# A streaming encoder on one core: the band's far corner masked by added contraction rows, turns over all 128 rows, and the bias reversed beside the latent heads

## The chip, the core and the metric

The kernel runs on one core of a Trainium2 chip. Its engines work side by side: TensorE (PE, with its weight loads PEld), VectorE (DVE), ScalarE (ACT), GpSimd (POOL) and SyncE (SP, which here issues every DMA). Each has its own instruction stream, and they order each other by semaphores. The metric is the time of one execution in microseconds of device time.

## The reference

One inference step of a two-layer trunk, for 1024 prompt frames and 64 sample frames that share all weights (model width 1024, chunks of 64 frames). The first layer runs two head groups from one projection: an mLSTM matrix memory (4 heads of 128) and a latent attention (8 heads). The second layer runs band attention with 16 heads of 64. Each layer ends in a SwiGLU FFN. What the change touches is in the band attention and, for the reversed bias, beside the latent attention:

```
def band_attend(q, k, v, q_pos, k_pos, rel_bias):
    s = einsum('bqhd,bkhd->bhqk', q, k) * C_SCALE
    idx = clip(q_pos[:, None] - k_pos[None, :], -MAX_REL, MAX_REL) + MAX_REL
    s = s + rel_bias[:, idx]
    qc, kc = (q_pos // CHUNK)[:, None], (k_pos // CHUNK)[None, :]
    valid = (k_pos[None, :] >= 0) & (kc <= qc) & (kc >= qc - LEFT_CHUNKS)
    p = softmax(where(valid, s, -inf))
    return einsum('bhqk,bkhd->bqhd', p, v)
```

With chunks of 64 and 8 chunks to the left, a tile of 128 queries sees five tiles of 128 keys, and in the farthest one the corner of the second 64 queries against the first 64 keys is outside the band: the far corner. It exists for query tiles 4 to 7.

## The kernel before, in words

The program is a row of stages (`load`, `in0`, `gate`, `mlstm`, `latent`, `heads`, `mla`, `out0`, `ffn0`, `in1`, `band`, `out1`, `ffn1`, `final`); a stage ends with its semaphores cleared and a barrier of all engines, and each stage holds one hand-written instruction stream per engine. Order within a stage is the order of these streams, and their waits.

**Latent attention (`mla_stage`).** Eight heads, nine query tiles each (`TILES`), in pairs: pair 0 written out, pairs 1 and 2 in a loop, pair 3 written out. For each tile PE scores, DVE takes the maximum, ACT exponentiates, PE turns the weights, ACT keeps them, PE weighs V. SP's stream loads q and k of the first two heads (`load(0)`, `load(1)`), then per head the V of the next head (`load_v`), and, after ACT, DVE and POOL have split the next head's q and k (`wait_split`), the q and k of the head after that. ACT's `split_q` (L1562) is the first that waits for such a load; it stands in ACT's stream between the exponentials. At the end of SP's stream `turn_bias` (L1365) copies the relative bias reversed into `relT` (L1369, one element at a time in reverse order), waits for it, spreads it into `biasT` (L1372), and waits for that.

**Band attention (`band_stage`).** Sixteen heads; those of a pair share 128 output rows, e = h % 2. A head has 13 pieces (`PIECES`, index i): eight key tiles against the queries that see them, cut at 512 queries, and the sample last. Key-major scores of a piece are two matmuls, `k2` by `q2` over 128 rows and `k3` by `q3` over H + 1 = 65 rows (row 64 carries a one against the negative row maximum), then two matmuls with `biasT`, and, in pieces i = 5, 7, 9 and 11, one matmul over a single row of `halves` that puts the mask on the far corner (L1925). ACT exponentiates a piece (L2022; the sample in two, L2017 and L2019), and PE weighs V with it two pieces later (L1948; the sample L1943, whose last key tile has 64 rows).

The row maxima of the next head are found beside the pieces of this one: at i = 4 to 12 PE computes the scores of query tile t = i - 4 once more, query-major, in `peak` (L1869; for tiles 4 to 7 with a one-row `halves` matmul for the corner), and DVE reduces them (L2099). `peak(h, t)` waits until DVE has reduced tile t - 1. PE then turns the maxima into rows (`rows`, L1888, the sample's over 64 rows) and ACT writes them into row 64 of `q3` (`keep_row`). PE also turns the next head's V (L1822), K (L1832, five turns over 64 rows, and the sample's V, L1833) and cached K (L1838); ACT takes the K (`take_k`) before PE may turn the cache. DVE has, in between, the divisions of the heads of the pair before or of this one (`divide`, L2114 a reciprocal and L2117 a product; `QUOTIENT_AT` places four of them at i = 7 to 10 of odd heads and five at i = 3, 5, 7, 9, 11 of even heads), `split_q`, `take_v` (L2089), `split_c` and `keep_tot`. At the stage's start DVE fills constants (eight instructions, `set_up`), and PE waits for them before the first `peak`.

In fp32 a matmul leaves two weight loads and two matmul records in the trace; a transpose leaves one of each.

## Time and profile before

| what | value |
|---|---|
| median of three runs | 3591.8 us (3588.12 to 3599.15) |
| the profiled execution: its time, its span | 3594.18 us, 3592.4 us |
| PE busy over the span | 3259.7 us (91%) |
| DVE, ACT, POOL busy | 1100.4, 888.6, 918.5 us (31%, 25%, 26%) |
| mean granted TensorE clock | 0.948 of full speed |

The span runs from the first to the last instruction of the profiled execution; its time has 1.8 us more. A PE record starts when the engine takes it up and its end is modelled, so the distance from one start to the next says more than the duration. The number in brackets at the end of a row is idle time of that engine before the instruction, with what ended it; "issue" is idle time in which the engine waited for nothing that the profile shows.

### The profile page before, as it was taken

How to read it: one execution, taken by the hardware profiler on the slowest of the kernel's cores; microseconds unless marked ns; L12 is line 12 of the kernel's file. 1: busy time of each engine (PE TensorE's matmuls, PEld its weight loads, DVE VectorE, ACT ScalarE, POOL GpSimd, SP SyncE). 2: the span in 40 equal slices, each digit the busy share in tenths (PEclk: the TensorE clock that was granted, in tenths of full speed). 3: DMA queues.
4: the chain of work that ended last, by engine and by line, in shares of the span. 5: the costliest groups of instructions: out<-in, count | busy, mean ns of one | idle time of the engine just before them, and what ended most of it. 6: DMA issues, size and time to landing. Idle time of an engine off the chain costs nothing. (4 is left out here: it accounts for less than half of the span.)

```text
span 3592.4 us, 49644 instructions
## 1 busy us (share of the span) xinstructions
PE 3259.7 (91%) x19284; PEld 3070.4 (85%) x19284; DVE 1100.4 (31%) x2155; ACT 888.6 (25%) x1626; POOL 918.5 (26%) x604
## 2 busy tenths in 40 slices
PE   6996558899889999999989997999988999999998
PEld 5996337788879999999979995777777999999998
DVE  3112662454131221222141113555522212211223
ACT  3001422554131221212130002444322212111211
POOL 3211102110142322232232113444313323222320
PEclk8998678899989999999999997999989999999999
DMA  3222414315121111111002215334312111111101
GB/s 105 97 90 101 109 47 163 77 47 52 47 70 36 59 47 35 35 58 47 0 30 95 92 73 137 81 79 85 76 36 70 48 35 37 56 47 35 47 23 56
DMA packets 194784, 229.78 MB, mean 64 GB/s; under 512 B 61631, under 2 KB 167312, under 8 KB 194464
## 3 DMA queue, kind: packets, MB, share of 16 engines
q1 hardware_dynamic: 194688, 228.51, 22.3%
q8 instruction: 60, 0.98, 0.1%
q14 instruction: 36, 0.29, 0.0%
HBM read 181.92 MB, written 54.44 MB: 66 GB/s over the span
## 5 line engine op out<-in xcount | busy, mean ns | idle before, releaser
L237 PE MATMUL ffn_banks<-hhi,ffn_whi 128*128 128x384 f32 (+1 forms) x2112 | 691.6, 327 | 20.2 <-POOL hlo L218 13.2
L239 PE MATMUL ffn_banks<-hhi,ffn_wlo 128*128 128x384 f32 (+1 forms) x2112 | 691.2, 327 | 0.0
L238 PE MATMUL ffn_banks<-hlo,ffn_whi 128*128 128x384 f32 (+1 forms) x2112 | 691.1, 327 | 0.0
L237 PEld LDWEIGHTS ffn_banks<-hhi,ffn_whi 128*128 128x128 f32 x2112 | 399.1, 189 | 21.7 <-issue 21.7
L238 PEld LDWEIGHTS ffn_banks<-hlo,ffn_whi 128*128 128x128 f32 x2112 | 398.9, 189 | 0.0
L239 PEld LDWEIGHTS ffn_banks<-hhi,ffn_wlo 128*128 128x128 f32 x2112 | 398.7, 189 | 0.0
L891 POOL TENSOR_TENSOR ffn_wlo<-ffn_stage,ffn_whi 128x2048 fp32r<-128x2048 f32 x66 | 303.5, 4611 | 357.8 <-ACT ffn_whi L851 357.8
L237 PE MATMUL in_banks<-hhi,in_whi 128*128 128x384 f32 (+1 forms) x1104 | 362.8, 329 | 22.5 <-issue 13.6
L957 DVE TENSOR_TENSOR ffn_act<-ffn_silu,ffn_banks 128x384 f32<-128x384 f32 x132 | 70.1, 532 | 962.7 <-PE ffn_banks L239 946.3
L239 PE MATMUL in_banks<-hhi,in_wlo 128*128 128x384 f32 (+1 forms) x1104 | 362.3, 328 | 0.0
L238 PE MATMUL in_banks<-hlo,in_whi 128*128 128x384 f32 (+1 forms) x1104 | 362.0, 328 | 0.0
L963 DVE TENSOR_TENSOR xT<-xT,ffn_banks 128x384 f32<-128x384 f32 (+1 forms) x528 | 281.0, 532 | 240.4 <-PE ffn_banks L239 240.4
L239 PE MATMUL ffn_banks<-ffn_ahi,ffn_wlo 128*128 128x384 f32 (+1 forms) x1056 | 344.2, 326 | 0.0
L238 PE MATMUL ffn_banks<-ffn_alo,ffn_whi 128*128 128x384 f32 (+1 forms) x1056 | 344.1, 326 | 0.0
L237 PE MATMUL ffn_banks<-ffn_ahi,ffn_whi 128*128 128x384 f32 (+1 forms) x1056 | 344.0, 326 | 0.0
L898 POOL TENSOR_TENSOR ffn_alo<-ffn_act,ffn_ahi 128x384 fp32r<-128x384 f32 x132 | 128.2, 972 | 792.8 <-ACT ffn_ahi L863 792.8
L237 PEld LDWEIGHTS in_banks<-hhi,in_whi 128*128 128x128 f32 x1104 | 209.1, 189 | 24.7 <-issue 14.6
L320 POOL TENSOR_TENSOR in_wlo<-in_stage,in_whi 128x1024 fp32r<-128x1024 f32 x46 | 109.7, 2386 | 455.4 <-ACT in_whi L298 455.4
L859 ACT ACTIVATE ffn_silu<-ffn_banks 128x384 f32<-128x384 f32 x132 | 62.4, 474 | 621.0 <-PE ffn_banks L239 621.0
L365 DVE COPY in_rows<-in_banks 128x384 f32<-128x384 f32 x138 | 73.9, 536 | 462.3 <-PE in_banks L239 462.3
L851 ACT ACTIVATE ffn_whi<-ffn_stage 128x2048 fp32r<-128x2048 f32 x66 | 124.1, 1909 | 363.6 <-PE ffn_banks L239 358.4
L238 PEld LDWEIGHTS in_banks<-hlo,in_whi 128*128 128x128 f32 x1104 | 209.0, 189 | 0.0
(306 smaller groups left out, 5386.1 us busy)
## 6 DMA issues: line engine op xcount, KB each, us to landing
park_z<-in_rows SPq DMA_DIRECT2D x46, 544.0 KB
ffn_stage<-in_w_gate SPq DMA_DIRECT2D x22, 1024.0 KB
ffn_stage<-in_w_up SPq DMA_DIRECT2D x22, 1024.0 KB
ffn_stage<-in_w_down SPq DMA_DIRECT2D x22, 1024.0 KB, 4.9
in_stage<-in_w_qkv SPq DMA_DIRECT2D x12, 1024.0 KB
in_stage<-in_w_in SPq DMA_DIRECT2D x11, 1024.0 KB
band_q_in<-park_z SPq DMA_DIRECT2D x32, 272.0 KB
band_k_in<-park_z SPq DMA_DIRECT2D x32, 272.0 KB
```

Source lines behind the costliest of these rows:

```text
L237: nc.tensor.matmul(out, whi[:, k, :], hhi[:, k, c0:c0 + w], start=(k == 0), stop=False)
L238: nc.tensor.matmul(out, whi[:, k, :], hlo[:, k, c0:c0 + w], start=False, stop=False)
L239: last = nc.tensor.matmul(out, wlo[:, k, :], hhi[:, k, c0:c0 + w], start=False, stop=(k == kts - 1))
L320: nc.gpsimd.tensor_tensor(wlo[:, h], stage[:, :, h * P:(h + 1) * P], whi[:, h], ALU.subtract).then_inc(lo_done, 1)
L365: nc.vector.tensor_copy(rows[:, h, c0:c0 + w], banks[:, b, 0:w]).then_inc(emptied, 1)
L851: nc.scalar.activation(whi[m][:], stage[m][:], ACT.Copy).then_inc(w_hi[m], 1)
L859: nc.scalar.activation(silu[:, f, 0:w], banks[:, 2 * f, 0:w], ACT.Silu).then_inc(silu_done, 1)
L891: nc.gpsimd.tensor_tensor(wlo[m][:], stage[m][:], whi[m][:], ALU.subtract).then_inc(w_lo[m], 1)
L898: nc.gpsimd.tensor_tensor(alo[:, f, c0:c0 + w], act32[:, f, 0:w], ahi[:, f, c0:c0 + w], ALU.subtract).then_inc(a_lo, 1)
L957: nc.vector.tensor_tensor(act32[:, f, 0:w], silu[:, f, 0:w], banks[:, 2 * f + 1, 0:w], ALU.mult).then_inc(product, 1)
L963: nc.vector.tensor_tensor(x, x, banks[:, 4 + k % 4, 0:w], ALU.add).then_inc(added, 1)
```

## The change

The one-row `halves` matmuls go. In the scores, `k3` and `q3` grow from 65 to 69 contraction rows: rows 65 to 68, one for each of the query tiles 4 to 7, carry the mask on the keys of the far half tile and a one on the queries of that tile's second half. In `peak` the corner is masked by a matmul of `ident` by `corner` over 128 rows. The five turns of K become plain matmuls of `k_in` (both halves of its 128 rows hold the same data) by the first 64 columns of the identity. The sample's maxima are turned, and its last key tile weighed, over 128 rows; the sample's exponential becomes one instruction. DVE's set-up grows from 8 to 43 instructions, and ACT waits for it too, before its first row of maxima. In the latent attention's SP stream the reversed copy is issued after `load(1)`, and its spread into `biasT` before the last two heads.

```diff
@@ -1362,15 +1362,19 @@
                     dve.tensor_tensor(dst, dst, turned[:, c0:c0 + w], ALU.add).then_inc(s["dve_kept"], 1)
 
 
-def turn_bias(nc, sp, D, bias_in):
+def reverse_bias(nc, sp, D, bias_in):
 
     rel, n = D["rel"], D["rel"].shape[1]
     back = bass.AP(rel.tensor, n - 1, [[n, C_HEADS], [-1, n]])
     sp.dma_start(D["relT"], back, allow_slow_non_contiguous=True).then_inc(bias_in, 16)
+
+
+def turn_bias(nc, sp, D, bias_in):
+
+    n = D["rel"].shape[1]
     sp.wait_ge(bias_in, 16)
     rows = bass.AP(D["relT"].tensor, P - 1, [[n, C_HEADS], [-1, P], [1, 2 * P]])
     sp.dma_start(D["biasT"], rows).then_inc(bias_in, 16)
-    sp.wait_ge(bias_in, 32)
 
 
 def mla_stage(nc, S, D):
@@ -1471,12 +1475,14 @@
             load_v(0, 0)
             wait_split(0)
             load(1)
+            reverse_bias(nc, sp, D, s["bias_in"])
             with sp.Fori(0, pairs - 1) as hp:
                 for e in range(2):
                     head(hp, e, False)
+            turn_bias(nc, sp, D, s["bias_in"])
             for e in range(2):
                 head(pairs - 1, e, True)
-            turn_bias(nc, sp, D, s["bias_in"])
+            sp.wait_ge(s["bias_in"], 32)
 
         @block.tensor
         def _(pe):
@@ -1692,17 +1698,21 @@
 def band_stage(nc, S, D):
 
 
+
     H = C_DIM
     CT = PAST_LEN // P
     VT = NT + CT
     LOADS, STORES = 11, 4
     HALF = 512
+    FAR = range(4, SEQ // P)
+    R = H + 1 + len(FAR)
 
     BLOCKS = [[0, 1, 2, 3], [4, 3, 5, 2, 6, 1, 7, 0], [None]]
     PIECES = [(b, j) for b, js in enumerate(BLOCKS) for j in js]
     N = len(PIECES)
     SAMPLE = N - 1
     LAG = 2
+    SET_UP = 2 * (8 + 3 * len(FAR)) + 3
     RING = 3
 
     PEAK_AT = {4 + t: t for t in range(NT)}
@@ -1739,7 +1749,7 @@
         c_in = st.sb("c_in", [P, CT, 2, H])
         b_in, bT_in = st.sb("b_in", [P, 2 * P]), st.sb("bT_in", [P, 2 * P])
         q2, k2 = st.sb("q2", [P, 2, NT * P], F32R), st.sb("k2", [P, 2, KEYS], F32R)
-        q3, k3 = st.sb("q3", [H + 1, 2, T], F32R), st.sb("k3", [H + 1, 2, KEYS], F32R)
+        q3, k3 = st.sb("q3", [R, 2, T], F32R), st.sb("k3", [R, 2, KEYS], F32R)
         V = st.sb("V", [P, 2, VT, P])
         ktok = st.sb("ktok", [P, 5, H])
         near = st.sb("near", [P, 2, 2 * P], F32R)
@@ -1749,7 +1759,7 @@
         p = st.sb("p", [P, RING, HALF])
         neg_max = st.sb("neg_max", [P, 2, NT])
         num, tot = st.sb("num", [P, T]), st.sb("tot", [P, T])
-        halves = st.sb("halves", [1, 2 * P + CHUNK], F32R)
+        corner = st.sb("corner", [P, CHUNK], F32R)
         pS = st.ps("pS", [P, RING, HALF])
         pM = st.ps("pM", [P, 2, HALF])
         pO = st.ps("pO", [P, 2, HALF])
@@ -1829,7 +1839,7 @@
                     pe.wait_ge(s["v_taken"], 1)
                 for q, c in enumerate(range(4, NT)):
                     w = tile_width(c)
-                    nc.tensor.transpose(spare[0:w, q * H:(q + 1) * H], k_in[0:H, c * P:c * P + w], S["ident"][0:H, 0:H])
+                    nc.tensor.matmul(spare[0:w, q * H:(q + 1) * H], k_in[:, c * P:c * P + w], S["ident"][:, 0:H], start=True, stop=True)
                 nc.tensor.transpose(spare[0:DEC_SEQ, 5 * H:6 * H], v_in[:, SEQ:T], S["ident"][0:H, 0:H]).then_inc(s["k_turned"], 1)
 
             def turn_c(h):
@@ -1859,8 +1869,8 @@
                 width, b0 = (P, P) if t == 0 else (192, 0) if t == NT - 1 else (2 * P, 0)
                 for i, (c, k0, kw) in enumerate(runs):
                     parts = [(out[:, c:c + kw], q2[:, e, qs], k2[:, e, k0:k0 + kw])]
-                    if i == 0 and 4 <= t < NT - 1:
-                        parts.append((out[:, c:c + CHUNK], halves[0:1, P:2 * P], halves[0:1, 2 * P:2 * P + CHUNK]))
+                    if i == 0 and t in FAR:
+                        parts.append((out[:, c:c + CHUNK], ident[:], corner[:]))
                     lo_, hi_ = max(c, end - width), c + kw
                     if lo_ < hi_:
                         b = b0 + lo_ - (end - width)
@@ -1884,8 +1894,7 @@
                     pe.wait_ge(s["row_kept"], 3 * h + 2)
                     pe.wait_ge(s["maxed"], NT * h + 9)
                 for q, t in enumerate((range(0, 4), range(4, 8), range(8, 9))[r]):
-                    w = tile_width(t)
-                    ins = nc.tensor.transpose(spare[0:1, q * P:q * P + w], neg_max[0:w, e, t:t + 1], S["ident"][0:w, 0:w])
+                    ins = nc.tensor.transpose(spare[0:1, q * P:q * P + P], neg_max[:, e, t:t + 1], S["ident"][:])
                 ins.then_inc(s["row_turned"], 1)
 
             def group(dst, parts):
@@ -1921,8 +1930,6 @@
                     if b0 < 2 * P:
                         bw = min(w, 2 * P - b0)
                         parts += [(slice(0, bw), ident[:], biasT[:, e, part, b0:b0 + bw]) for part in range(2)]
-                    if q0 + w == (j + 5) * P:
-                        parts.append((slice(w - CHUNK, w), halves[0:1, 0:P], halves[0:1, 2 * P:2 * P + CHUNK]))
                     ins = group(dst, parts)
                 ins.then_inc(s["scored"], 1)
 
@@ -1939,8 +1946,8 @@
                     pe.wait_ge(s["tot_out"], G - 1)
                 pe.wait_ge(s["exped"], g + 1)
                 if i == SAMPLE:
-                    for c, (_, kw, vt) in enumerate(key_tiles(NT - 1)):
-                        ins = nc.tensor.matmul(pO[:, G % 2, 0:CHUNK], V[0:kw, e, vt, :], p[0:kw, g % RING, c * CHUNK:(c + 1) * CHUNK],
+                    for c, (_, _, vt) in enumerate(key_tiles(NT - 1)):
+                        ins = nc.tensor.matmul(pO[:, G % 2, 0:CHUNK], V[:, e, vt, :], p[:, g % RING, c * CHUNK:(c + 1) * CHUNK],
                                                start=(c == 0), stop=(c == CT))
                 else:
                     q0, w = span_of(b, j)
@@ -1952,7 +1959,7 @@
             turn_v(0)
             turn_k(0)
             turn_c(0)
-            pe.wait_ge(s["set_up"], 8)
+            pe.wait_ge(s["set_up"], SET_UP)
             for t in range(NT):
                 peak(0, t)
             rows(0, 0)
@@ -2013,13 +2020,8 @@
                 act.wait_ge(s["scored"], g + 1)
                 if g >= RING:
                     act.wait_ge(s["summed"], g - RING + 1)
-                if i == SAMPLE:
-                    act.activation(p[0:DEC_SEQ, g % RING, CT * CHUNK:(CT + 1) * CHUNK],
-                                   pS[0:DEC_SEQ, g % RING, CT * CHUNK:(CT + 1) * CHUNK], ACT.Exp)
-                    act.activation(p[:, g % RING, 0:CT * CHUNK], pS[:, g % RING, 0:CT * CHUNK], ACT.Exp).then_inc(s["exped"], 1)
-                else:
-                    w = span_of(b, j)[1]
-                    act.activation(p[:, g % RING, 0:w], pS[:, g % RING, 0:w], ACT.Exp).then_inc(s["exped"], 1)
+                w = (CT + 1) * CHUNK if i == SAMPLE else span_of(b, j)[1]
+                act.activation(p[:, g % RING, 0:w], pS[:, g % RING, 0:w], ACT.Exp).then_inc(s["exped"], 1)
 
             def keep_num(h, b):
                 e, G = h % 2, 3 * h + b
@@ -2036,6 +2038,7 @@
             split_q(0)
             take_k(0)
             split_c(0)
+            act.wait_ge(s["set_up"], SET_UP)
             keep_row(0, 0)
             for h in range(C_HEADS):
                 for i in range(N):
@@ -2067,12 +2070,27 @@
 
         @block.vector
         def _(dve):
-            ones = lambda r, n: S["ones"][r, 0:H].rearrange("p (a n) -> p a n", a=1).to_broadcast([1, n, H])
+            low_rows = slice(H, R)
+            unit = lambda i, n: S["ident"][low_rows, i:i + 1].to_broadcast([R - H, n])
+            far_rows, one_row = S["ident"][low_rows, H:H + 1], slice(0, FAR[0] * P)
             for e in range(2):
-                dve.tensor_copy(k3[H:H + 1, e, :].rearrange("p (a n) -> p a n", n=H), ones(slice(H, H + 1), KEYS // H)).then_inc(s["set_up"], 1)
+                odd = k3[low_rows, e, one_row].rearrange("p (t a n) -> p t a n", a=2, n=CHUNK)[:, :, 1, :]
+                dve.tensor_copy(odd, far_rows.rearrange("p (a n) -> p a n", a=1).to_broadcast([R - H, len(FAR), CHUNK])).then_inc(s["set_up"], 1)
+                dve.tensor_copy(k3[low_rows, e, FAR[0] * P:KEYS], unit(H, KEYS - FAR[0] * P)).then_inc(s["set_up"], 1)
+                for i, t in enumerate(FAR):
+                    j = t - FAR[0]
+                    dve.tensor_scalar(k3[low_rows, e, j * P:j * P + CHUNK], unit(H + 1 + i, CHUNK), NEG, far_rows, ALU.mult, ALU.add)\
+                       .then_inc(s["set_up"], 1)
+                    dve.tensor_copy(q3[low_rows, e, t * P:t * P + CHUNK], unit(0, CHUNK)).then_inc(s["set_up"], 1)
+                    dve.tensor_copy(q3[low_rows, e, t * P + CHUNK:(t + 1) * P], unit(H + 1 + i, CHUNK)).then_inc(s["set_up"], 1)
+                dve.tensor_copy(q3[low_rows, e, 0:FAR[0] * P], unit(0, FAR[0] * P)).then_inc(s["set_up"], 1)
+                dve.tensor_copy(q3[low_rows, e, SEQ:T], unit(0, DEC_SEQ)).then_inc(s["set_up"], 1)
                 dve.memset(V[:, e, :, own(1 - e)], 1.0).then_inc(s["set_up"], 1)
+                dve.memset(V[DEC_SEQ:P, e, NT - 1, own(e)], 1.0).then_inc(s["set_up"], 1)
                 dve.tensor_scalar(q2[:, e, T:NT * P], S["ones"][:, 0:NT * P - T], 0.0, None, ALU.mult).then_inc(s["set_up"], 1)
-            dve.tensor_copy(halves[:], S["halves"][:]).then_inc(s["set_up"], 1)
+                dve.memset(neg_max[DEC_SEQ:P, e, NT - 1:NT], 0.0).then_inc(s["set_up"], 1)
+            dve.tensor_copy(corner[0:CHUNK], S["ident"][0:CHUNK, CHUNK:P]).then_inc(s["set_up"], 1)
+            dve.tensor_scalar(corner[CHUNK:P], S["ones"][CHUNK:P, 0:CHUNK], NEG, None, ALU.mult).then_inc(s["set_up"], 1)
             dve.tensor_copy(ident[:], S["ident"][:]).then_inc(s["set_up"], 1)
 
             def split_q(h):
```

## Rows read from the trace of the kernel before

**Rows 1.** Busy time by window: PE, PEld, DVE, ACT, POOL, clock, DMA share, GB/s.

```profile
842.00:850.00 8.00, 6.94 (x51) 6.21 (x50) 6.48 (x11) 4.38 (x11) 3.58 (x1) 1.00 1.96 16
...
2155.00:2193.00 38.00, 15.30 (x51) 10.09 (x51) 14.45 (x20) 2.92 (x7) 14.98 (x12) 0.50 0.83 211
2228.00:2630.00 402.00, 373.74 (x2160) 295.29 (x2159) 218.70 (x347) 164.53 (x431) 157.98 (x163) 0.98 0.38 77
```

**Rows 2.** Timeline of PE, one odd band head: start us, us, engine, line, operation.

```profile
2340.26 0.21 PE L1888 MATMUL band_spare<-ident,band_neg_max 64*1 64x64 f32 x1 [1.06 <-DVE band_V L2089]
2340.58 1.10 PE L1948 MATMUL band_pO<-band_p,band_V 128*128 128x512 f32 x2
...
2342.00 0.51 PE L1832 MATMUL band_spare<-ident,band_k_in 64*128 64x64 f32 x5
2342.36 0.22 PE L1833 MATMUL band_spare<-ident,band_v_in 64*64 64x64 f32 x1
...
2357.59 0.29 PE L1893 MATMUL band_pS<-band_halves 1*128 1x64 f32 x1
2357.82 0.39 PE L1869 MATMUL band_pM<-band_k,band_q 128*128 128x256 f32 x1
2358.14 0.29 PE L1869 MATMUL band_pM<-band_halves 1*128 1x64 f32 x1
2358.36 0.44 PE L1869 MATMUL band_pM<-band_k,band_q 128*128 128x384 f32 x1
...
2360.68 0.48 PE L1869 MATMUL band_pM<-band_k,band_q 128*128 128x256 f32 x2
```

**Rows 3.** Timeline of DVE, the same head: maxima of tiles 3, 5, 6, 7.

```profile
2350.35 0.69 DVE L2099 TENSOR_REDUCE band_neg_max<-band_pM 128x1 f32<-128x512 f32 x1 [0.71 <-PE band_pM L1869]
...
2354.64 0.83 DVE L2099 TENSOR_REDUCE band_neg_max<-band_pM 128x1 f32<-128x640 f32 x1
...
2356.66 0.82 DVE L2099 TENSOR_REDUCE band_neg_max<-band_pM 128x1 f32<-128x640 f32 x1
...
2358.96 0.82 DVE L2099 TENSOR_REDUCE band_neg_max<-band_pM 128x1 f32<-128x640 f32 x1 [0.29 <-PE band_pM L1869]
```

**Rows 4.** Timeline of PE, latent attention: a 64-row turn; a group resumed.

```profile
844.43 1.36 PE L1517 MATMUL mla_pP<-mla_diag,mla_p 64*128 64x64 f32 x10
...
869.67 1.87 PE L1533 MATMUL mla_pO<-mla_pT,mla_V 128*128 128x128 f32 x8 [5.75 <-issue]
```

**Rows 5.** Timeline of DVE, start of the band stage.

```profile
2155.43 1.81 DVE L2072 CAST band_k<-ones 1x1600 fp32r<-1x1600 f32 x1 [3.73 <-PEq L64]
...
2168.40 1.29 DVE L2080 SCALAR_TENSOR_TENSOR band_q<-band_q_in,band_q 64x1088 fp32r<-64x1088 f32 x1 [6.53 <-ACT band_q L1988]
```

**Rows 6.** Timeline of PE, start of the band stage: the first turns of K.

```profile
2170.47 0.79 PE L1832 MATMUL band_spare<-ident,band_k_in 64*128 64x64 f32 x5 [2.08 <-DVE band_V L2089]
```

**Rows 7.** Timeline of ACT, latent attention: one tile's exponential, heads 5, 6, 7.

```profile
828.00 1.11 ACT L1572 ACTIVATE mla_p<-mla_pS,mla_neg_max 128x1024 f32<-128x1024 f32 x1 [2.29 <-DVE mla_neg_max L1638]
...
858.95 1.11 ACT L1572 ACTIVATE mla_p<-mla_pS,mla_neg_max 128x1024 f32<-128x1024 f32 x1 [2.44 <-DVE mla_neg_max L1638]
...
896.69 1.11 ACT L1572 ACTIVATE mla_p<-mla_pS,mla_neg_max 128x1024 f32<-128x1024 f32 x1 [2.30 <-DVE mla_neg_max L1638]
```

**Rows 8.** Timeline of SP, latent attention: DMA issues.

```profile
644.80 0.47 SPq L1448 DMA_DIRECT2D mla_k_in<-park_heads_k  x1
...
663.38 0.47 SPq L1445 DMA_DIRECT2D mla_q_in<-park_heads_q  x1
...
839.97 0.64 SPq L1369 DMA_DIRECT2D park_relT<-in_rel  x1
872.78 0.54 SPq L1372 DMA_DIRECT2D park_biasT<-park_relT  x1
```

**Rows 9.** Timeline of ACT, latent attention: split_q of heads 1 and 2.

```profile
649.97 1.10 ACT L1562 ACTIVATE mla_qhi<-mla_q_in 96x1088 fp32r<-96x1088 f32 x1
...
683.98 1.10 ACT L1562 ACTIVATE mla_qhi<-mla_q_in 96x1088 fp32r<-96x1088 f32 x1
```

## The prediction, made before the change was run

> **What bounds the kernel now.** I read the page first, then the busy time by windows, then the timelines of PE, DVE, ACT and SP around the places that the diff touches. In the steady part of the band stage PE is busy for 373.74 of 402 us, 93%, at a clock of 0.98, that is the 2.4 GHz level; DVE is busy for 218.70 [rows 1]. So PE's stream sets the pace there, but not everywhere. Two places in a head show PE waiting for others. Before it turns the sample's maxima it is idle for 1.06 us, released by DVE's copy of V [rows 2]. And while it recomputes the tiles of the next head, DVE's maxima of tiles 5 and 6 follow each other in 2.02 us (2354.64 to 2356.66), neither with idle time in front of it [rows 3]: a maximum (0.82) and a division fill DVE there, so in that stretch DVE is the bound and PE happens to be as slow. The maximum of tile 7 has 0.29 us of idle time before it, released by PE [rows 3]: there PE is late.
>
> In the latent attention the thing to see is one stall. PE resumes at 869.67 after 5.75 us for which the profile shows no releaser, in the middle of a group of weighings that has no wait inside [rows 4]. The same exponential comes 30.95 us after that of the head before in one case (828.00 to 858.95) and 37.74 us after it in the next (858.95 to 896.69) [rows 7]: the stall and what follows from it cost 6.79 us. It falls into the 32.8 us between the issue of the reversed copy at 839.97 and that of its spread at 872.78, which waits for it [rows 8]. In that time the DMA engines show a share of 1.96 and move only 16 GB/s [rows 1].
>
> **The change part by part.**
>
> **1. The reversed copy moves.** Its old place costs 6.79 us. With the copy at about 645, that stretch keeps only the spread, which is then issued before the last two heads; it was in flight from 872.78 on without a stall that I can find behind it. I take -6.8. SP's final wait costs nothing before or after: the spread is issued at 872.78 and the last head's work goes on past 896.69 [rows 7, 8]. In its new place the copy stands in SP's queue behind `load(1)`, whose last issue is at 644.80, and ahead of all later loads of V, q and k. ACT takes up q of head 1 at 649.97 with no idle time noted before it [rows 9], so `load(1)` has at most 5.2 us. In the old place the V of the last head was issued just ahead of the copy and no later row waits for it, so I price `load(1)` at +0.3 (bounds 0 and the whole copy, 32.8 less 4.7 = 28).
>
> The Trainium skill (DMA: Bandwidth & Descriptors, "Queues, rings and completion order") says that an engine consumes its descriptors in ring order and that a completion counts only after that engine's earlier writes. No row of the trace before has a load behind the copy. By that rule the loads of head 2, issued at 663.38, could not be counted before the copy has landed at about 645 + 33 = 678, and are wanted at 683.98: in time if they need no more than the 5.2 us of `load(1)`, but 4.5 us late (678 + 5.2 + 5.2 = 688.5) if the V queued before them takes as long again; the sum would then be -13.7 in place of -18.2.
>
> The same skill (Runtime: NRT & Kernel Launch, "Instruction fetch mechanics") says that a sequencer fetches its instructions by DMA in pages while it executes. The stall in mid-group with no releaser is what that would look like when the fetch is held up; the sum does not rest on it.
>
> **2. The score masks go.** A one-row matmul holds PE from its start to the next start for 0.23 us (2357.59 to 2357.82) [rows 2]; what it holds up ahead of it comes on top, so I take 0.25 for each of the four in a head: 1.0 us of PE. The grown contraction, 69 rows for 65, keeps the instructions and their columns: 0.
>
> **3. The peak masks change form.** From the first matmul of a tile over the one-row matmul to the third it is 0.54 us (2357.82, 2358.14, 2358.36) [rows 2]. A record pair over many rows with 64 columns costs 0.12: ten of them take 1.36, less about 0.25 for the end of the last, over nine distances [rows 4]. So 256 columns and the corner should take about 0.27 to 0.29; I take 0.25 saved, four times in a head: 1.0 us of PE.
>
> **4. The turns of K.** Five one-record turns take 0.36 from start to the next start [rows 2]. As plain fp32 matmuls they leave ten records at 0.12: 1.2. That is +0.84 per head. The sample's V still turns over 64 rows behind them, so the switch is not saved, only moved. Bounds: ten records at 0.07, the price of today's turns, +0.35; ten at 0.14, +1.0. They are exposed: ACT takes K only after the last turn, and PE's next work waits for ACT.
>
> **5. The sample's maxima over 128 rows.** From this turn to the next start it is 0.32 (2340.26 to 2340.58) [rows 2]; at 0.12 for a full one, -0.2, and exposed, since PE waited just before. The sample's weighing over 128 rows stands ahead of that 1.06 us wait, whose end is DVE's, at the end of a chain that starts with ACT's exponential of piece 0; what PE saves there (0.2 to 0.3) makes it wait longer: 0. ACT's single exponential of the sample hides in the same way, ACT being busy for 41% of the stretch [rows 1]: 0.
>
> **6. Set-up.** DVE starts at 2155.43 and its next real work, at 2168.40, comes after 6.53 us idle [rows 5]. The 1600-column fill takes 1.81. The new 43 instructions fill some 3,650 columns in each of the two buffers and 256 more: at 1.13 ns a column 8.5 us, and 13.0 are there. That leaves 0.1 us of overhead for each instruction; I take it as hidden. At 0.2 each it would run over by 4, with every engine behind it: +4 is the bound. PE's first turns of K are exposed at a clock of 0.50, the 1.2 GHz level [rows 1]: five take 0.79 [rows 6]; ten records at twice 0.12 make about 2.4, so +1.7. The first head's four peaks alternate with DVE and save at least 0.25 each: -1.0. Sum of the start: +0.7.
>
> **7. What a head gains.** PE's savings are 1.0 + 1.0 + 0.2 - 0.84 = 1.36, but DVE decides how much of it counts. The longer turns less the sample's turn shift the tiles by +0.64; the two score masks ahead of tile 3 (i = 5 and 7) take back 0.5, which leaves +0.1. From the maximum of tile 3 (2350.35) on, DVE has one division in each gap. Its own pace is 2.02 per gap, and 1.89 for the first, whose maximum is 0.69 long. So tile 6's maximum cannot come earlier than 5.93 after tile 3's; it came after 6.31 [rows 3]. That is 0.38 less 0.1: 0.28. PE started tile 7 1.16 us after that maximum began (2357.82 against 2356.66) [rows 2, 3]; with its masks gone it starts when the maximum is done, after about 0.88: 0.28 more. From tile 7 to tile 8 (2357.82 to 2360.68) one mask of 0.2 to 0.25 goes [rows 2]. Sum 0.76. Even heads have a division only in every other gap but one more in front; I take 0.76 for them too. Fifteen heads prepare a next one: -11.4. The last head has no peaks and gains its four score masks: -1.0.
>
> Sum: -6.8 + 0.3 + 0.7 - 11.4 - 1.0 = **-18.2 us**. The profiled execution took 3594.18 us, 2.4 above the median of the three; taken from the median 3591.8 that is 3573.6, so I predict **3574 us**.
>
> **The rivals.**
>
> *PE gains all it saves.* If the divisions don't bind in even heads and the waits shift with PE, the heads give 15 x 1.36 = 20.4 in place of 11.4: about 3564. Against it stand the two maxima without idle time [rows 3].
>
> *The stall moves with the copy.* What held PE for 5.75 us is held up at 645 to 680 instead, or the loads of head 2 come late. Either gives back 5 to 7 us: about 3580. For it speaks that the same copy shows its 32.8 us again; against it, that the loads have some 20 us (663.38 to 683.98) [rows 8, 9]. The two rules of the skill named above both point this way.
>
> *Slower: `load(1)` is caught.* If the copy holds up `load(1)` until it has landed, ACT stands at `split_q` from 649.97 to about 678, and with it every later exponential: +28, so 3592 - 18 + 28 = 3602. It decides as soon as the wait exceeds the 18 us won elsewhere. Against it: in 842 to 850 the engines move 16 GB/s [rows 1], so the V issued just ahead of the copy was through.
>
> *The band gains nothing.* The turns of K at their upper price (+1.0) and DVE binding in even heads as hard as in odd ones leave some 0.2 a head; only the stall and the last head's masks are left: about 3582 to 3586.
>
> **Numbers.** The forecast gets 0.48, full gain 0.10, the moved stall 0.20, the caught load 0.06, no gain in the band 0.16. The likeliest case alone spans 3567 to 3580 (the turns at either bound make 15 x 0.16 more or 15 x 0.5 less, the fills up to 4 more). To leave out no more than 2 in 10, the range goes from 3561 to 3587. A measurement of this kernel can tell about 0.3%, 11 us: below 3581 is faster. That holds for nearly all of the first two cases and half of the third, and little of the last: 0.68. Within 0.3%: 0.24. Slower: the caught load and a little more, 0.08.
>
> **What would show it.** After: no PE row with 5.75 us of "issue" in the latent attention, 31 us between the same exponentials in all heads, and ACT's `split_q` of heads 1 and 2 with no idle time from a DMA. In the band: no one-row records, 0.28 from the first to the third matmul of a far tile, ten records for the turns of K with 1.2 us between their start and that of the sample's V, more idle time of PE before the maxima of tiles 5 to 7, and a distance between equal places of two neighbouring heads that is 0.76 us shorter. The prediction is wrong if a DMA releases ACT near 650 or 684, if that distance shrinks by less than 0.2 or by over 1.2, or if DVE's set-up takes over 13 us.

## The result and the profile after

The changed kernel takes 3623.99 us (median of four runs, 3618.6 to 3626.25) against 3593.16 of the kernel before: a ratio of 1.0083, 95% interval 1.0063 to 1.0103. It is slower by 31 us, where 18 us faster was forecast. Its profiled execution took 3622.8 us, with a span of 3621.0 and a mean granted clock of 0.933.

The busy time by windows of the changed kernel, columns as in [rows 1]: first the three stretches of [rows 1], then two heads of the band (from one of DVE's copies of V to the next), then four stretches inside them.

```profile
842.00:850.00 8.00, 7.99 (x58) 7.41 (x59) 5.45 (x13) 6.31 (x16) 1.95 (x1) 1.00 0.37 105
2155.00:2193.00 38.00, 19.62 (x76) 14.64 (x76) 14.06 (x40) 6.56 (x11) 19.11 (x13) 0.50 0.76 197
2228.00:2630.00 402.00, 369.39 (x1974) 295.95 (x1974) 195.23 (x314) 148.37 (x373) 148.71 (x150) 0.83 0.38 76
...
2372.68:2403.78 31.10, 28.30 (x151) 22.60 (x151) 15.38 (x26) 11.37 (x29) 11.58 (x13) 0.84 0.37 75
2403.78:2434.11 30.33, 28.06 (x151) 22.60 (x151) 14.49 (x24) 11.35 (x28) 11.26 (x12) 0.83 0.38 77
...
2384.10:2404.50 20.40, 18.37 (x120) 15.17 (x119) 13.57 (x21) 8.99 (x21) 8.10 (x8) 1.00 0.47 91
2404.50:2414.80 10.30, 9.59 (x31) 7.13 (x32) 0.32 (x2) 1.71 (x7) 2.95 (x4) 0.50 0.16 43
2414.80:2435.30 20.50, 18.87 (x123) 15.70 (x123) 14.61 (x24) 9.78 (x23) 8.78 (x8) 1.00 0.48 92
2435.30:2445.50 10.20, 9.51 (x32) 7.17 (x32) 1.37 (x3) 2.23 (x9) 2.99 (x5) 0.50 0.20 44
```

PE is as busy as before in the steady part (369 of 402 us), but at a clock of 0.83 and not 0.98 [rows 1]. The last four lines show why: in each head some 20 us at the 2.4 GHz level are followed by 10 us at the 1.2 GHz level. The kernel before does the same, but seldom. Three windows of it: a head without such a fall, a head with one, and the fall itself.

```profile
2366.75:2394.36 27.61, 25.42 (x150) 20.11 (x150) 15.55 (x26) 11.43 (x31) 11.58 (x13) 1.00 0.42 85
2394.36:2424.36 30.00, 28.13 (x150) 22.25 (x150) 14.76 (x24) 11.28 (x30) 11.28 (x12) 0.89 0.38 78
...
2396.40:2403.20 6.80, 6.12 (x26) 4.87 (x24) 0.29 (x1) 1.55 (x6) 1.64 (x3) 0.50 0.28 74
```

From the first copy of V to the last it is 421.95 us before (2169.72 to 2591.67) and 453.17 after (2165.24 to 2618.41): 31.2 us more, the whole loss. Of the last 13 of these 15 heads, 2 fall before and 13 after; their mean goes from 27.83 to 30.65 us. The first two heads together are 5.4 us shorter, since the clock of the stage's start rises sooner (head two, from 2198.82 before and 2194.31 after, has a clock of 0.84 before and 1.00 after).

The timeline of PE around one fall (answers [rows 2]):

```profile
2401.32 1.33 PE L1950 MATMUL band_pO<-band_p,band_V 128*128 128x64 f32 x10
2402.46 0.48 PE L1902 MATMUL band_pS<-band_q,band_k 128*128 128x256 f32 x2
...
2404.53 0.37 PE L1897 MATMUL band_spare<-ident,band_neg_max 128*1 128x128 f32 x1 [1.34 <-DVE band_V L2107]
2404.84 2.05 PE L1955 MATMUL band_pO<-band_p,band_V 128*128 128x512 f32 x2
...
2407.43 2.31 PE L1842 MATMUL band_spare<-ident,band_k_in 128*128 128x64 f32 x10
2409.68 0.31 PE L1843 MATMUL band_spare<-ident,band_v_in 64*64 64x64 f32 x1
```

The same wait as in [rows 2] is there, 1.34 us in place of 1.06, and the clock falls at its end. What follows is the serial part of a head: a weighing with pairs of 512 columns takes 2.05 and not 1.10, the turns of K 2.25 from start to start.

DVE, the maxima of tiles 3, 5, 6 and 7 in the same head as in [rows 3], and the end of the set-up with the first real work (answers [rows 5]):

```profile
2160.86 0.23 DVE L2094 CAST band_ident<-ident 128x128 fp32r<-128x128 f32 x1
2163.92 1.29 DVE L2098 SCALAR_TENSOR_TENSOR band_q<-band_q_in,band_q 64x1088 fp32r<-64x1088 f32 x1 [2.83 <-ACT band_q L1995]
...
2357.49 0.69 DVE L2117 TENSOR_REDUCE band_neg_max<-band_pM 128x1 f32<-128x512 f32 x1 [0.28 <-PE band_pM L1879]
...
2361.28 0.82 DVE L2117 TENSOR_REDUCE band_neg_max<-band_pM 128x1 f32<-128x640 f32 x1
...
2363.20 0.82 DVE L2117 TENSOR_REDUCE band_neg_max<-band_pM 128x1 f32<-128x640 f32 x1
...
2365.12 0.82 DVE L2117 TENSOR_REDUCE band_neg_max<-band_pM 128x1 f32<-128x640 f32 x1
```

From tile 3 to tile 7 it is 7.63 us (8.61 in [rows 3]), with steps of 1.92 and no idle time: DVE is the bound there. So what the masks should give is given, and the fall takes it back. The set-up is hidden, with 2.83 us to spare.

In the latent attention, SP's issues, then ACT's exponentials of one tile in the first two heads and the last two (answer [rows 7, 8]), and then ACT's `split_q` of heads 1 and 2 (answer [rows 9]) with PE's two stops between these heads:

```profile
625.82 0.52 SPq L1449 DMA_DIRECT2D mla_q_in<-park_heads_q  x1
...
640.96 0.62 SPq L1369 DMA_DIRECT2D park_relT<-in_rel  x1
645.98 17.52 SPq L1457 DMA_DIRECT2D mla_V<-park_heads_v  x2
664.04 6.01 SPq L1459 DMA_DIRECT2D mla_V<-park_heads_v  x1
```

```profile
668.26 1.11 ACT L1578 ACTIVATE mla_p<-mla_pS,mla_neg_max 128x1024 f32<-128x1024 f32 x1 [2.44 <-DVE mla_neg_max L1644]
...
706.79 1.11 ACT L1578 ACTIVATE mla_p<-mla_pS,mla_neg_max 128x1024 f32<-128x1024 f32 x1 [2.32 <-DVE mla_neg_max L1644]
...
861.67 1.11 ACT L1578 ACTIVATE mla_p<-mla_pS,mla_neg_max 128x1024 f32<-128x1024 f32 x1 [2.46 <-DVE mla_neg_max L1644]
...
891.53 1.11 ACT L1578 ACTIVATE mla_p<-mla_pS,mla_neg_max 128x1024 f32<-128x1024 f32 x1 [2.29 <-DVE mla_neg_max L1644]
```

```profile
648.36 1.11 ACT L1568 ACTIVATE mla_qhi<-mla_q_in 96x1088 fp32r<-96x1088 f32 x1 [2.65 <-DMA mla_k_in<-park_heads_k]
...
675.56 0.37 PE L1539 MATMUL mla_pO<-mla_pT,mla_V 128*128 128x128 f32 x1 [1.56 <-issue]
...
680.95 3.49 PE L1539 MATMUL mla_pO<-mla_pT,mla_V 128*128 128x128 f32 x16 [2.70 <-issue]
...
686.67 1.10 ACT L1568 ACTIVATE mla_qhi<-mla_q_in 96x1088 fp32r<-96x1088 f32 x1
```

The last two are 29.86 apart (37.74 in [rows 7]): the old stall is gone. But the first two are 38.53 apart. SP is held for 17.52 and 6.01 us in issuing V behind the copy, yet ACT does not wait for head 2's load (686.67). It waits 2.65 us for head 1's, which was issued ahead of the copy and for which it had not waited before [rows 9]; and PE stands twice with "issue", 1.56 and 2.70 us, as it stood 5.75 us at the old place [rows 4]. The stage as a whole, from its first load to the first load of `out0`, takes 274.6 us both times (before 631.02 to 905.59, after 625.82 to 900.43).

### The profile page after: what moved, and what is told of

Same layout as the page of the kernel before. It is cut to its first block and busy times, and to the rows that moved or that the text cites. A ratio compares the mean times of both kernels' runs of the same rounds, so it can differ in the third digit from the quotient of the medians.

```text
span 3621.0 us, 49696 instructions
## 1 busy us (share of the span) xinstructions
PE 3285.4 (91%) x19300; PEld 3096.7 (86%) x19300; DVE 1099.8 (30%) x2190; ACT 888.1 (25%) x1610; POOL 917.8 (25%) x604
```

## The experiments

**The theories.** A: PE's wait for DVE's copy of V, in a light stretch (matmuls of 64 columns, turns, one-column turns of maxima), brings the clock down once in a head, and the change made the dense rest of the head so short that it does so in each. K: the turns of K as ten records do it; W: the wider sample work does it; P: any new length of a head moves the falls. For the bias, S: the move saves its 6.8 us; M: the move is itself what made the kernel slower. The expectations are those put down before each run.

The heads of each kernel, from the windows between DVE's copies of V in its one profiled execution; "13 heads" are the last 13 of the 15 distances, and a head has fallen if its granted clock is below 0.95. The ratio is to the kernel before as it was run beside each group of runs, where its median was 3591.6 to 3597.0 us; medians of different groups can differ by as much for that reason alone.

| kernel | median, ratio to before (95%) | 13 heads, mean us | fallen | mean without, with a fall |
|---|---|---|---|---|
| before | 3593.2 | 27.83 | 2 | 27.44, 30.01 |
| changed | 3624.0, 1.0083 (1.0063 to 1.0103) | 30.65 | 13 | none, 30.65 |
| 1 copy put back | 3632.9, 1.0099 (1.0082 to 1.0116) | 30.72 | 13 | none, 30.72 |
| 2 K transposed | 3585.2, 0.9961 (0.9933 to 0.9990) | 28.12 | 9 | 25.53, 29.27 |
| 3 masks alone | 3600.9, 1.0016 (1.0006 to 1.0025) | 28.82 | 12 | 25.85, 29.06 |
| 4 wait filled | 3570.6, 0.9920 (0.9903 to 0.9936) | 26.38 | 0 | 26.38, none |
| 5 V early | 3555.1, 0.9886 (0.9869 to 0.9902) | 25.37 | 0 | 25.37, none |
| 6 before, V early | 3587.9, 0.9974 (0.9964 to 0.9983) | 27.69 | 4 | 26.54, 30.26 |
| 7 filled elsewhere | 3613.7, 1.0050 (1.0033 to 1.0067) | 28.62 | 5 | 26.90, 31.38 |
| 8 K turns alone | 3648.5, 1.0135 (1.0114 to 1.0155) | 32.11 | 12 | 28.45, 32.42 |
| 9 V early, K transposed | 3536.9, 0.9850 (0.9837 to 0.9864) | 24.89 | 1 | 24.57, 28.73 |
| 10 as 9, copy put back | 3537.6, 0.9855 (0.9838 to 0.9872) | 24.55 | 0 | 24.55, none |
| 11 as 9, copy forward | 3527.6, 0.9820 (0.9806 to 0.9833) | 24.54 | 0 | 24.54, none |
| 12 masks alone, V early | 3555.3, 0.9899 (0.9882 to 0.9917) | 25.22 | 2 | 24.71, 28.02 |
| 13 K turns alone, wait filled | 3605.2, 1.0035 (1.0024 to 1.0047) | 28.26 | 0 | 28.26, none |
| 14 before, wait filled | 3592.9, 1.0000 (0.9990 to 1.0010) | 28.03 | 2 | 27.42, 31.37 |
| 15 sample as before | 3624.6, 1.0089 (1.0073 to 1.0106) | 30.70 | 13 | none, 30.70 |

**1. The copy put back**, on the changed kernel:

```diff
-            reverse_bias(nc, sp, D, s["bias_in"])
             with sp.Fori(0, pairs - 1) as hp:
...
-            turn_bias(nc, sp, D, s["bias_in"])
             for e in range(2):
                 head(pairs - 1, e, True)
+            reverse_bias(nc, sp, D, s["bias_in"])
+            turn_bias(nc, sp, D, s["bias_in"])
```

> The changed kernel with the reversed copy of the bias back behind the last latent head; everything in the band as changed. Theory A (the loss of 31 us is all in the band, because the clock falls to its 1.2 GHz level once in every head; the copy's move only carried its stall from one place to the other): the 5.75 us stall of PE near 870 is back, the late loads of head 2 near 676 are gone, the latent stage takes the same 274.6 us, the band's heads still take 30.7 us, and the total stays at 3624 give or take 4. Rival M (the move of the copy is what made the kernel slower): at least 7 us faster, 3617 or less. Rival S (the move saved the 6.8 us and the band lost more): at least 6 us slower, 3630.

3632.9 us. The heads are the same, 13 fallen, so the move did not bring the clock down (rival M falls). In absolute time it fits rival S, but the intervals of the two ratios overlap, and the profile puts the 9 us elsewhere: the latent stage takes 276.25 us, 1.6 more than in the changed kernel; it starts 6.9 us later (632.75 for 625.82), ahead of anything this edit touches; and the band's 15 heads take 458.04 us for 453.17. In the stage PE's stop is back (7.12 us, up to 872.36), and ACT no longer waits for head 1's load.

**2 and 3. One part back, one part alone.** Run 2 has this edit on the changed kernel; run 3 has it too, and the copy and the sample's work as before, so that the masks alone are left:

```diff
-                    nc.tensor.matmul(spare[0:w, q * H:(q + 1) * H], k_in[:, c * P:c * P + w], S["ident"][:, 0:H], start=True, stop=True)
+                    nc.tensor.transpose(spare[0:w, q * H:(q + 1) * H], k_in[0:H, c * P:c * P + w], S["ident"][0:H, 0:H])
```

> The changed kernel with the turns of K as transposes again (five records in place of ten). Theory A (the clock falls because the rest of the stream became shorter and lighter ahead of PE's wait for DVE's copy of V): the clock still falls in most heads, a head loses the 1.0 us that ten records take at the lower level more than five do, so between 29.5 and 30.7 us a head and 3606 to 3624 in all. Rival K (the longer turns of K themselves are the cause: the chain from the sample's row turn to peak 0 became 0.84 us longer and that brings the clock down): the clock stays at 2.4 GHz in nearly all heads, 26 to 27 us a head, 3555 to 3575 in all.

> The masks of the far corner alone are changed (69 contraction rows, the corner as a matmul over 128 rows, with their set-up); the turns of K, the sample's weighing, its exponential and its row turn, and the place of the reversed copy are as before. Theory A (what matters is that PE's stream between two waits for DVE's copy of V became shorter): the clock falls in most heads here too, 29.5 to 31 us a head, 3605 to 3625. Rival K or W (the turns of K, or the sample's weighing and row turn over 128 rows, bring it down): the clock falls no more often than before, in 2 or 3 heads, and the masks' gain is seen: 25.5 to 26.7 us a head, 3565 to 3585.

Run 2 lies between the theories: 9 heads fall, at 29.27, and 4 do not, at 25.53. The turns of K matter, but the clock falls without them. Its median fits neither theory (3606 to 3624, or 3555 to 3575). Run 3 bears out theory A in the falls: with the masks alone 12 heads fall; its mean head and its median lie just below what A gave. A fallen head there costs less, 29.06. Its one head without a fall (2252.20 to 2278.05) takes 25.85 us; the same head before takes 27.62 (2257.06 to 2284.68): at the upper level the masks are worth 1.77 us.

**4. The wait filled**, on the changed kernel:

```diff
                 else:
+                    pe.wait_ge(s["maxed"], NT * h + 9)
+                    for _ in range(5):
+                        nc.tensor.matmul(pM[:, 0, :], ident[:], k2[:, e, 0:HALF], start=True, stop=True)
                     if h + 1 < C_HEADS:
                         pe.wait_ge(s["v_taken"], h + 2)
                     pe.wait_ge(s["row_kept"], 3 * h + 2)
-                    pe.wait_ge(s["maxed"], NT * h + 9)
```

> The changed kernel with five matmuls of 512 columns that nobody reads, put in front of PE's wait for DVE's copy of V (about 1.1 us at the upper level, inside the 1.34 us that PE stands there), into the bank of the peaks, which is free then. Nothing else changes, and no other engine waits for them. Theory A (the light stretch with this wait brings the clock down): the clock stays at 2.4 GHz, the heads go from 30.7 to about 26 us, and the total from 3624 to 3550 to 3560. Rival K (the stream behind the wait is the cause): the clock falls as often, the added matmuls cost 0 to 1 us a head: 3624 to 3640. Rival P (any change of the head's length moves the drop): some heads fall and some do not, between 3560 and 3624.

3570.6 us, 53 us less than the changed kernel, by work that nobody needs; theory A had 3550 to 3560, so the total missed while the heads came as expected. PE's timeline at the wait, and a window of one head:

```profile
2386.73 1.32 PE L1894 MATMUL band_pM<-band_k,band_ident 128*128 128x512 f32 x5
2388.22 0.27 PE L1899 MATMUL band_spare<-ident,band_neg_max 128*1 128x128 f32 x1 [0.17 <-DVE band_V L2109]
2388.54 1.10 PE L1957 MATMUL band_pO<-band_p,band_V 128*128 128x512 f32 x2
```

```profile
2360.82:2387.48 26.66, 25.17 (x158) 20.29 (x158) 15.41 (x26) 11.35 (x29) 11.57 (x13) 1.00 0.43 88
```

The wait for DVE ends as before; only what PE does in it has changed. None of the 13 heads falls, and they take 26.38: the fall costs 30.65 less 26.38, 4.27 us a head, if the five matmuls cost nothing. For that speaks run 2, whose heads without a fall, 25.53, make 26.35 with the 0.82 us of the turns of K (run 13). Rival K falls for this kernel; of P what it forecast, falls in some heads, did not come.

**5 and 6. The wait taken away.** DVE's stream in step i = 1 and 2, on the changed kernel (5) and on the one before (6):

```diff
+                    if h and i == 1:
+                        keep_tot(h - 1, 1)
+                    if h + 1 < C_HEADS:
                         if i == 1:
+                            take_v(h + 1)
                             split_q(h + 1)
-                        if i == 2:
-                            take_v(h + 1)
...
-                    if h and i in (1, 2):
-                        keep_tot(h - 1, i)
+                    if h and i == 2:
+                        keep_tot(h - 1, 2)
```

> The changed kernel with a new order in DVE's stream alone: the copy of V and the first copy of the totals are taken ahead of DVE's split of q, for both of which their inputs are ready then, so that PE's wait of 1.34 us before the sample's row turn should be gone. Theory A (this wait, in a light stretch, brings the clock down): no drop in the heads, a head at 26.4 us (that of the kernel with the wait filled) less up to 1.3, so 25.1 to 26.4, and 3545 to 3570 in all. Rival K (the stream behind the wait is the cause): drops go on, only the wait is won, 29.4 us a head, about 3604. Rival D (DVE's later split of q delays peak 0 by as much): 26 us a head, a wait before peak 0.

> The same new order of DVE's stream in the kernel before, nothing else. Theory A: its 1.06 us wait goes, 15 x 1.06 = 16 us, and its two drops of the steady part with it, 5 us: 3572 to 3580. If the divisions on DVE take the gain back, or if the shorter head makes the clock fall more often: no gain, 3590 to 3600.

Run 5: 3555.1 us, no fall, 25.37 a head. PE's wait is 0.3, and it does not wait before peak 0, so rival D falls too. DVE's timeline in the new order:

```profile
2398.01 0.68 DVE L2126 COPY band_tot<-band_pO 64x512 f32<-64x512 f32 x1 [0.91 <-PE band_pO L1955]
2400.72 0.69 DVE L2107 COPY band_V<-band_spare 128x512 f32<-128x512 f32 x1 [2.03 <-PE band_pO L1950]
2401.45 2.96 DVE L2098 SCALAR_TENSOR_TENSOR band_q<-band_q_in,band_q 64x1088 fp32r<-64x1088 f32 x1
```

Run 6 is a miss. Its heads without a fall are 0.9 us shorter, as expected, but 4 of 13 fall, though PE's wait for V has gone down to 0.2. So the wait is not the only light work there: on the kernel before, the stretch around it is enough at times.

**7. The same matmuls elsewhere**, on the changed kernel, the wait left as it was:

```diff
+                        if i == 8:
+                            pe.wait_ge(s["c_hi"], h + 2)
+                            pe.wait_ge(s["c_lo"], h + 2)
+                            for _ in range(5):
+                                nc.tensor.matmul(spare[:], ident[:], k2[:, h % 2, 0:HALF], start=True, stop=True)
```

> The changed kernel with the same five matmuls of 512 columns per head, but in the dense part of a head (at piece 8, into the bank of the turned K, which is free then), with the wait for the copy of V left as it is. Theory A (what PE does just before and in the wait counts): the drop comes back in every head, the matmuls cost up to 1.1 us a head: 30.7 to 31.8 us a head, 3624 to 3640. Rival P (the drop hangs only on how the length of a head falls on the times at which the clock is set): the pattern changes, drops in some heads only, 3580 to 3620.

5 of 13 heads fall. The waits of PE, and two windows, a head without a fall and one with:

```profile
PE band_spare L1897 <- DVE band_V L2112: 17.5, 14, 1.3
```

```profile
2351.18:2377.87 26.69, 24.50 (x156) 20.34 (x156) 14.57 (x23) 11.35 (x28) 11.29 (x12) 1.00 0.43 88
2377.87:2409.48 31.61, 28.91 (x156) 23.22 (x156) 15.38 (x25) 11.38 (x29) 11.56 (x13) 0.84 0.37 74
```

The wait is in every head (14 times, 17.5 us), yet only some fall. That is a miss of theory A alone, and what rival P forecast. From here the theory is A+P: the light stretch is needed, and which heads fall hangs on their length as well. That it is the length, and not the added work as such, this run does not show: it changed both.

**8 and 13. The turns of K alone**, the edit of run 2 the other way round on the kernel before, and then with four matmuls in the wait as in run 4:

> The kernel before with the turns of K as ten records, nothing else. By the price of the prediction a head is 0.84 us longer: 28.3 us, 3595 + 13 = 3608, with as few drops as before. Rival K (the turns of K bring the clock down by themselves): a drop in every head, 30.7 us a head, 3640 or more. Rival P (each change of length moves the drops): some heads with a drop and some without, in between.

> The kernel before with the turns of K as ten records, and four matmuls of 512 columns that nobody reads put in front of PE's wait for DVE's copy of V (about 0.87 us inside its 1.06). Theory A+P (the light stretch with the wait is needed for the fall; the turns of K only change the head's length, and so on which heads it falls): no drops, heads of 28.3 us as in the undisturbed ones of the kernel with the turns of K alone (28.06 and 28.45), about 3648 - 13 x 4.1 = 3595, between 3590 and 3605. Rival K (the turns of K, ten short records of 64 columns, bring the clock down by themselves): drops go on, 3645 or more.

One small edit, 0.83 us of work a head, costs 52 us: 3648.5 for the 3597.0 of the kernel before beside it. Alone, this looked like rival K. Run 13 keeps the ten records and fills the wait: 3605.2, no fall. Windows of both, the two heads of run 8 that stand side by side with and without a fall, and one of run 13:

```profile
2229.30:2261.75 32.45, 30.59 (x155) 24.08 (x155) 14.75 (x23) 11.27 (x30) 11.22 (x12) 0.84 0.37 72
2261.75:2290.20 28.45, 26.26 (x155) 20.91 (x155) 15.55 (x25) 11.44 (x31) 11.57 (x13) 1.00 0.40 82
```

```profile
2255.08:2283.60 28.52, 27.30 (x162) 21.59 (x161) 15.56 (x25) 11.40 (x31) 11.58 (x13) 1.00 0.41 82
```

So K falls as a cause by itself: with the wait filled the same ten records run without a fall. Whether they bring on the 12 falls of run 8 by a head's length, as P has it, or as more light work behind the wait, is not shown. A fall costs 32.42 less 28.26, 4.2 us, with them, and 30.01 less 27.44, 2.6 us, in the kernel before; it also lasts longer, 10.2 us (2230.50 to 2240.74) for 6.8 (the last window of the kernel before above).

**14. The control**, the kernel before with the same four matmuls in the wait:

> The kernel before with the same four matmuls in front of the same wait. Theory A+P: its two drops of the steady part (2.6 us each) go and nothing else changes: 5 us less, 3583 to 3592. If the matmuls cost something in heads without a drop: the same or up to 10 us more.

The same time as before, 1.0000: not the 5 us less. The matmuls cost nothing (27.42 without a fall). One disturbance cost two heads. Its windows:

```profile
2400.00:2412.90 12.90, 12.90 (x69) 9.86 (x69) 10.13 (x16) 4.36 (x13) 1.83 (x4) 1.00 0.64 122
2412.90:2416.30 3.40, 3.40 (x16) 2.86 (x15) 0.75 (x1) 0.99 (x3) 3.39 (x3) 0.50 0.00 0
2416.30:2423.20 6.90, 4.79 (x35) 3.85 (x33) 5.00 (x5) 3.15 (x6) 6.75 (x5) 0.99 0.08 19
2423.20:2433.40 10.20, 9.52 (x30) 6.96 (x30) 1.41 (x3) 2.48 (x9) 0.79 (x2) 0.50 0.35 72
```

The clock fell at 2412.90 after a stretch in which PE was busy all the time (12.90 of 12.90), among them the sample's scores of 64 columns; then DVE's `split_q` took 3.35 us for 1.29, PE's wait grew to 2.00 behind the matmuls, and a second fall followed. Idle time alone does not decide.

The place does, nearly always. From the second copy of V to just behind the last, the clock falls 96 times in the 17 profiles. In 95 of them it does so between 0.72 us before and 1.25 us after the start of the sample's row turn, the first work behind PE's wait; so do the falls of runs 6, 9 and 12, where little of the wait is left. The first fall of run 14 is the 96th.

**15. The sample as before**, the changed kernel with narrow weighing, two exponentials and the 64-row turn:

> The changed kernel with the sample's weighing over its own rows, its two exponentials and its row turn over 64 rows as before; masks, turns of K and the copy's place as changed. The wait then is 1.08 in place of 1.34. Theory A+P: still a light stretch, drops in most or all heads, 30 to 31 us a head, 3615 to 3640. Rival W (the longer wait that the full rows make is what brings the clock down): few drops, 26.5 us a head, 3560 to 3580.

3624.6 us, 13 heads fallen with a wait of 1.1 us. The wider sample work is no cause (rival W falls).

**9 to 12. What each part is worth when the clock holds.** All with V early. Run 9 has the edits of runs 5 and 2; run 10 that of run 1 as well; run 11 is run 9 with a bias not reversed, so it does not compute the reference; run 12 is run 3 with V early.

```diff
-    back = bass.AP(rel.tensor, n - 1, [[n, C_HEADS], [-1, n]])
+    back = bass.AP(rel.tensor, 0, [[n, C_HEADS], [1, n]])
```

> The changed kernel with DVE's copy of V and of the totals ahead of its split of q, and the turns of K as transposes again. Theory A+P (a light stretch with PE's wait brings the clock down where the times at which the clock is set fall on it; without the wait there is nothing to fall on): no drop, and a head shorter by the 0.83 us that the turns of K cost at the upper level, 24.5 us in place of 25.4: 3540 to 3545. Rival P alone (any new length of the head can meet the times at which the clock is set, wait or no wait): drops in some heads, 3555 to 3585.

> The same with the reversed copy of the bias back behind the last latent head. With the clock steady in the band the copy's place can be read alone. As the prediction has it (the stall of 6.8 us is saved by the move): 6 to 7 us slower. Rival (the stall moves with the copy): the same within 3 us.

> The copy beside the latent heads, at its new place, takes the bias forward and not in reverse, in 16 rows of neighbouring elements (so the turned bias is that of a table not reversed, and the band's scores with it); all else as in the kernel with V early and K transposed. If the element-wise copy costs at its new place what the trace shows (SP held for 17.5 and 6.0 us behind it, head 2's loads late by 6.7 us for ACT): 6 to 7 us faster. If these waits are made up for later in the stage: the same within 2 us.

> The masks alone are changed, and V is taken early; turns of K, sample's weighing, exponential and row turn, and the place of the copy are as before. Beside the kernel with V early, K transposed and the copy back, it lacks only the sample's work over 128 rows. The prediction priced that at 0 for the weighing, since PE waited behind it, and 0.2 for the row turn. With the wait gone its saving shows: 0.3 to 0.5 us a head, so this one is 4 to 8 us slower than that. If the clock still falls in it: 10 to 40 slower.

Run 9 is the fastest that computes the reference, 3536.9 us, 1.5% below the kernel before; one of its 13 heads still fell, after a wait of 0.30, where theory A+P had none. Runs 9 and 10 are the same within 1 us, each ratio with an interval of 5 to 6 us to either side: the place of the copy is worth nothing that these two show. Run 11 is 9.3 us faster than run 9. About 4 of these may be the fall that run 9's profile has (28.73 against 24.57); in the latent stage run 11 takes 267.6 us (629.45 to 897.08), run 9 271.2: ACT's wait for head 1's load, 6.12 us in run 9, is gone. SP's issue of V behind the forward copy:

```profile
649.55 1.02 SPq L1457 DMA_DIRECT2D mla_V<-park_heads_v  x2
```

1.02 us in place of the 17.52 of the changed kernel: it is the element-wise reversal that holds SP. It also holds up the load issued just ahead of it: in the seven profiles with the reversed copy at its new place ACT waits 2.65 to 8.59 us for head 1's load (the least in the changed kernel), and in run 11 and the nine with the old place not at all. PE's stop, of 5.2 to 8.2 us near 870, is in the profiles of all nine; at the new place only the changed kernel has stops with "issue" of over 1 us. What makes PE stop is not shown. Over the profiles, the stage takes 271.2 to 282.0 us in the seven with the reversed copy at its new place (mean 274.7) and 273.8 to 277.8 in the nine with the old one (mean 275.9): 1.2 us between the means, and not the 6 to 7 of the forecast. Run 12 is 17.7 us behind run 10, more than the 4 to 8 expected, but two of its heads fell. Without falls the wider sample work is worth 24.71 less 24.55, 0.16 us a head, 2 in all, where 0.3 to 0.5 a head was expected.

## Why the prediction was wrong

**The step that failed is part 7, what a head gains.** It counted PE's and DVE's durations at the clock of the steady part, 0.98 [rows 1], as if that belonged to the stage. At the upper level it was right in kind and a little low: 27.44 to 26.38 (run 4) is 1.06 a head for the forecast 0.76. But all 13 heads fell, at 4.27 each. The mean of the 13 heads grew by 2.82 (30.65 less 27.83): 4.27 for the fall, less the 1.06 gained, less 0.39 that the two falls of the kernel before already cost (27.83 less 27.44). Times 13 that is 36.7, less the 5.4 of the first two heads: 31.3, the 31.2 of the trace but for rounding. Without the falls the kernel takes 3570.6 us (run 4), which lies in the forecast's range. That is partly luck: the gain from the copy did not come, and with the falls of the changed kernel those two of the kernel before, some 5 us, are gone as well.

The forecast had seen the wait of 1.06 us [rows 2], and it put the saving in front of it at nothing because it "makes it wait longer". It did not ask what PE's clock does in such a stretch, nor read the windows head by head. There two of the last 13 heads of the kernel before show 0.89 and 30.0 us beside 1.00 and 27.6 at most, so that the clock falls in some heads, and what a fall costs there, could have been read before. The Trainium skill ("TensorE: Matmul & The Clock Gate", "HAM oscillation — how this bites in real kernels") describes a loop in which the waits between bursts of matmuls bring the clock down in each pass. This trace agrees in form: one fall in each head. It differs in that PE waits only 1.34 us here, and that in run 14 the clock fell in a stretch without idle time.

The other parts:

- *The reversed copy, -6.8 and +0.3.* Part 1 failed too, in the +0.3 for `load(1)`. The old stall is gone (29.86 for 37.74), the new place costs as much (38.53 for the usual 31), and runs 9 and 10 show no difference. Of the rivals, the caught `load(1)` came true in kind, with waits of 2.65 to 8.59 us and not 28 (a DMA that releases ACT near 650 is one of the signs that the prediction named); the stall that moves came true in the changed kernel's profile alone. The rule of the Trainium skill that the prediction cited ("DMA: Bandwidth & Descriptors", "Queues, rings and completion order") bears on loads queued behind the copy. In the changed kernel ACT does not wait for these; the one it waits for was issued ahead of it, and SP's issues behind it themselves take 17.52 and 6.01 us.
- *The masks.* 1.77 us in the one head of run 3 without a fall, and 26.54 less 24.71, 1.83, between runs 6 and 12; part 7 comes to 1.40 (the 0.76 and the 0.64 of the turns), because it let DVE's divisions take more of the gain. DVE's own step is 1.92 us: the 2.02 read from [rows 3] held 0.10 of waiting that the rows do not mark.
- *The turns of K*, +0.84: 0.82 in run 13 (28.26 less 27.44) and 0.80 between runs 5 and 9. Right at the upper level. At the lower level the ten records take 2.31 us where five took 0.79 [rows 6], some 1.5 more.
- *The sample's rows*, -0.2: 0.16, read in kernels without the wait. Near.
- *The set-up*, hidden: right, with 2.83 us left. The first turns of K at the lower level took 2.30 for the estimated 2.4.

What stays open: which heads fall. No kernel whose wait of 1.0 us or more was left as it was is free of falls; with the wait filled or taken away 0 to 4 heads of 13 fall. Runs 7 and 8 show that about 1 us of other work in a head changes which heads fall; that the shorter dense part is why the change made all of them fall, as theory A has it, is argued and not shown by itself. The rule behind it was not found, and whether a still denser stretch would end all falls was not tried.

## What to carry to other kernels

Read the granted clock loop pass by pass before an edit is priced: where a few passes of the kernel before have fallen, an edit that shortens the stream (the change) or lengthens it (run 8) can make nearly all of them fall, and costs then more than it saves. Where PE waits in every pass, take the wait away first (here by the order of three instructions on DVE: run 5 is 69 us faster than the changed kernel), or fill it, and measure the edits after that. Moving the slow transfer moved its cost here; copying in order (run 11, which leaves the bias unreversed) took less.

## What the runs showed of the hardware

- Five matmuls that nobody reads, put into a wait of 1.34 us, made the kernel 53 us faster (run 4).
- A change of 0.83 us a head cost 52 us (run 8), and 0.82 a head when the wait was filled (run 13).
- Of 96 falls of the clock in the band's heads, 95 came within 0.72 us before and 1.25 us after the start of the same one-column turn (17 profiles).
- The clock fell once after 12.90 us in which PE had no idle time (run 14).
- Behind the reversed copy, SP's issue of two loads took 17.52 us; behind the same bytes in order, 1.02 us. The load issued ahead of it made ACT wait 2.65 to 8.59 us (seven profiles), ahead of the copy in order not at all.
- DVE's `split_q` took 2.96 us in its new place beside POOL's work (run 5) and 1.29 in its old one.
